# Feed-forwards of a retention and gated-delta trunk as 2x2x2 block products with seven products, down projection in four groups

## The chip, the cores and the metric

The kernel runs on one core of one Trainium2 chip. The metric is the device time of one execution in microseconds (us). A core has five engines that run their own instruction streams and wait for each other by semaphores: PE (TensorE, the matmuls), DVE (VectorE), ACT (ScalarE), POOL (GpSimd) and SP (SyncE, which here only issues DMAs). SBUF is the on-chip memory of 128 partitions, PSUM the eight accumulator banks that PE writes. All values are float32. A matmul here takes "fp32r" operands: each value is split into a high end, which is a rounded copy, and a low end, which is the value less that copy.

## What is computed

Two layers, each with two half-step SwiGLU feed-forwards around a mixer (retention in the first, gated delta rule in the second), on 520 tokens: 512 of a prompt and 8 samples. Cut to what matters here:

```python
D_MODEL, D_FF = 1024, 2816
def _swiglu(x, w_gu, w_down):
    a, b = jnp.split(x @ w_gu, 2, axis=-1)
    return (jax.nn.silu(a) * b) @ w_down
for i in range(DEPTH):                      # DEPTH = 2
    x = x + 0.5 * _swiglu(_rmsnorm(x, norm_g[i, 0]), ffn_gu[i, 0], ffn_down[i, 0])
    x = x + mixer(_rmsnorm(x, norm_g[i, 1]))    # retention, then gated delta
    x = x + 0.5 * _swiglu(_rmsnorm(x, norm_g[i, 2]), ffn_gu[i, 1], ffn_down[i, 1])
return _rmsnorm(x, final_g), states
```

## The kernel before

Activations lie transposed: model dimension on the partitions (8 tiles of 128), the 520 tokens along the row, in two halves of 260 (`HALF`). `plan()` lists ten phases in order: gate/up and down of feed-forward 0, retention, gate/up and down of feed-forwards 1 and 2, gated delta, gate/up and down of feed-forward 3. All engines walk this list; the order of their work is the order of the code.

Weights come in slots of at most 16 tiles of 128x128 (1 MB), two slots in turn. SP loads a slot into `raw`, ACT copies it to the high end `wh` (`split`, L1328, one instruction of 2048 columns, L1333), DVE subtracts to give the low end `wl` (`split`, L1669, L1672), and PE uses it. A slot of gate/up holds one gate tile column and one up tile column (8 tiles each), a slot of down holds half of a column of `w_down` (11 tiles, 1408 columns). So gate/up is 22 slots and down 16 slots a feed-forward.

On PE, `products` (L736) does for each weight tile three terms (high x high, high x low, low x high) for both halves of the tokens: six matmuls of 260 columns (L743), accumulated in two banks. That makes 22 x 96 + 8 x 132 = 3168 matmuls a feed-forward. After a gate and an up column DVE scales both by the norm's `rinv` (L2258), ACT applies Silu (L1632), DVE multiplies (L2261), ACT and DVE split the product into `hh` and `hl` (L1635, L2263). After a down column DVE adds into `x` (L2276), ACT and DVE make the next stage's scaled `xh` and `xl` (L1651, L1678), ACT squares (L1655) and POOL adds the squares (`sum_squares`, L548); the next stage's norm comes from that sum. POOL has no other work in the feed-forwards.

The mixers also use `split`, `products` and `in_products` (L934), and POOL does elementwise work in them: sums of squares (L588), masks and state decays (`add` in `gdn_body`, L643).

## Time and profile before

| | |
|---|---|
| median of 3 runs | 2621.64 us (2612.52 to 2621.98) |
| profiled execution, first to last instruction | 2619.2 us |
| PE busy | 2572.6 us, 98% of the span |
| DVE busy | 1264.2 us, 48% |
| ACT busy | 821.0 us, 31% |
| POOL busy | 300.5 us, 11% |
| mean granted PE clock | 0.990 of full speed |

The profiled execution is 2.4 us shorter than the median. Busy time of an engine is the union of its instructions. A timeline or chain row gives the start in us from the span's start, then its length in us. A row of a stretch gives busy us and instructions of PE, PEld (weight loads), DVE, ACT and POOL in that order. A row by line and form gives line, engine, operation, tiles, shapes and count, then busy us and the mean duration of one in ns, then the idle time before it and what ended most of it.

### The profile page before, as it was taken

The numbers are of one execution on the slowest core, as the hardware profiler recorded it, in microseconds if no ns is written. First come the engines' busy times: TensorE is split into PE (matmuls) and PEld (weight loads), VectorE is DVE, ScalarE is ACT, GpSimd is POOL, SyncE is SP. The second block draws the span as 40 slices with busy tenths as digits, with TensorE's granted clock in tenths as the row PEclk, the third lists the DMA queues.
The fourth block names the chain that finished last, engine by engine and source line by source line (L and its number), as shares of the span: only waits on it lengthen the run. The fifth ranks groups of instructions, "written<-read, shape, count | busy, mean of one in ns | idle before, by whom it ended". The sixth has DMA issues, their size and how long they took to land.

```text
span 2619.2 us, 48630 instructions
## 1 busy us (share of the span) xinstructions
PE 2572.6 (98%) x20575; PEld 2484.8 (95%) x20575; DVE 1264.2 (48%) x1584; ACT 821.0 (31%) x1042; POOL 300.5 (11%) x307
## 2 busy tenths in 40 slices
PE   8999999999999999999999999999999998999998
PEld 8999999898989899999999999989998998999998
DVE  5444334646464654443244443377557755444422
ACT  4222222424242432222232222244433344222222
POOL 1000010202020210000000000002530353000000
PEclk9999999999999999999999999999999999999999
DMA  4332334524242333332343323321122111323232
GB/s 131 96 96 76 88 93 141 185 86 177 93 173 97 137 91 87 96 86 78 97 111 91 96 82 89 104 84 52 49 66 87 36 49 53 97 84 93 78 91 74
DMA packets 340333, 246.73 MB, mean 94 GB/s; under 512 B 9428, under 2 KB 320908, under 8 KB 340208
## 3 DMA queue, kind: packets, MB, share of 16 engines
q1 hardware_dynamic: 325856, 197.32, 25.6%
q0 software_dynamic: 14352, 47.58, 5.0%
q8 instruction: 99, 1.62, 0.3%
q14 instruction: 26, 0.21, 0.0%
HBM read 218.81 MB, written 26.05 MB: 93 GB/s over the span
## 4 chain that ended last, share of the span: by engine, by line
PE 95%; DVE 3%; ACT 1%; issue 0%; DMA 0%; SPq 0%; ACTq 0%; DVEq 0%
PE ps L743 61%; PE ps L934 17%; PE ps L1118 5%; PE ps L828 1%; PE ps L851 1%; PE ps L837 1%; PE ps L1062 1%; PE ps L1128 1%; PE ps L783 1%; PE ps L1099 1%; DVE wl L1672 1%; PE ps L1075 1%; PE ps L993 0%; DVE xl L1678 0%; DVE cv L2012 0%
## 5 line engine op out<-in xcount | busy, mean ns | idle before, releaser
L743 PE MATMUL ps<-xh,wh 128*128 128x260 f32 x2816 | 569.0, 283 | 3.7 <-DVE gate L2258 1.5
L743 PE MATMUL ps<-xh,wl 128*128 128x260 f32 x2816 | 568.3, 284 | 0.0
L743 PE MATMUL ps<-xl,wh 128*128 128x260 f32 x2816 | 567.5, 283 | 0.0
L1672 DVE TENSOR_TENSOR wl<-raw,wh 128x2048 fp32r<-128x2048 f32 (+1 forms) x204 | 428.7, 2102 | 266.7 <-ACT wh L1333 266.5
L1333 ACT ACTIVATE wh<-raw 128x2048 fp32r<-128x2048 f32 (+1 forms) x204 | 354.5, 1738 | 343.2 <-PE ps L743 189.2
L743 PEld LDWEIGHTS ps<-xh,wh 128*128 128x128 f32 x2816 | 435.4, 189 | 5.8 <-issue 2.7
L743 PEld LDWEIGHTS ps<-xh,wl 128*128 128x128 f32 x2816 | 435.1, 189 | 0.0
L743 PEld LDWEIGHTS ps<-xl,wh 128*128 128x128 f32 x2816 | 433.8, 189 | 0.0
L743 PE MATMUL ps<-hh,wh 128*128 128x260 f32 x1408 | 284.4, 283 | 0.0
L743 PE MATMUL ps<-hh,wl 128*128 128x260 f32 x1408 | 283.1, 282 | 0.0
L743 PE MATMUL ps<-hl,wh 128*128 128x260 f32 x1408 | 282.8, 282 | 0.0
L934 PE MATMUL ps<-xh,wh 128*128 128x260 f32 x1280 | 271.1, 294 | 1.7 <-DVE rot L1727 0.8
L934 PE MATMUL ps<-xh,wl 128*128 128x260 f32 x1280 | 261.3, 286 | 0.0
L934 PE MATMUL ps<-xl,wh 128*128 128x260 f32 x1280 | 261.1, 286 | 0.0
L2258 DVE TENSOR_TENSOR up<-ps,rinv 128x520 f32<-128x520 f32 x88 | 61.5, 699 | 382.6 <-PE ps L743 382.6
L743 PEld LDWEIGHTS ps<-hl,wh 128*128 128x128 f32 x1408 | 217.1, 188 | 0.0
L743 PEld LDWEIGHTS ps<-hh,wl 128*128 128x128 f32 x1408 | 216.9, 188 | 0.0
L743 PEld LDWEIGHTS ps<-hh,wh 128*128 128x128 f32 x1408 | 216.6, 188 | 0.2
L934 PEld LDWEIGHTS ps<-xh,wh 128*128 128x128 f32 x1280 | 201.7, 193 | 15.5 <-issue 9.7
L1635 ACT ACTIVATE hh<-up 128x520 f32 (+1 forms) x88 | 56.3, 640 | 467.5 <-DVE up L2261 467.5
L934 PEld LDWEIGHTS ps<-xl,wh 128*128 128x128 f32 x1280 | 202.1, 193 | 0.0
L934 PEld LDWEIGHTS ps<-xh,wl 128*128 128x128 f32 x1280 | 202.0, 193 | 0.0
(372 smaller groups left out, 2857.8 us busy)
## 6 DMA issues: line engine op xcount, KB each, us to landing
raw<-in_ffn_gu_dram SPq DMA_DIRECT2D x176, 512.0 KB, 4.9
raw<-in_ffn_down_dram SPq DMA_DIRECT2D x64, 384.0 KB, 3.5
raw<-in_ret_w_in_dram SPq DMA_DIRECT2D x48, 512.0 KB, 4.4
raw<-in_ffn_down_dram SPq DMA_DIRECT2D x64, 320.0 KB, 3.9
s_ring<-in_state_ret_dram POOLq DMA_DIRECT2D x32, 512.0 KB, 6.2
out_dram<-s_ring POOLq DMA_DIRECT2D x32, 512.0 KB, 3.4
raw<-in_gdn_w_in_dram SPq DMA_DIRECT2D x32, 512.0 KB, 4.5
raw<-in_ret_w_out_dram SPq DMA_DIRECT2D x16, 512.0 KB, 3.8
```

Source lines behind the costliest of these rows:

```text
L743: m_ = nc.tensor.matmul(ps[:, 2 * q + h, 0:HALF], w_, v[:, kt0 + t, h * HALF:(h + 1) * HALF], start=b_, stop=e_)
L783: m_ = nc.tensor.matmul(o, rk[:, t, jb * P:(jb + 1) * P], rq[:, t, jb * P:SEQ], start=t == 0, stop=t == 1)
L828: m_ = nc.tensor.matmul(ps[:, 4 + e, jb * P:SEQ], vtok[:, jb, e * P:(e + 1) * P], pt[:, off[jb]:off[jb] + SEQ - P * jb], start=jb == 0, st ...
L837: m_ = nc.tensor.matmul(ps[:, 4 + t, :], ktok[:, jb, t * P:(t + 1) * P], vtok[:, jb, :], start=jb == 0, stop=jb == 3)
L851: m_ = nc.tensor.matmul(ps[:, 7, e * DEC + b:e * DEC + b + 1], weighed(b)[:, e * P:(e + 1) * P], ones[:, 0:1], start=True, stop=True)
L934: m_ = nc.tensor.matmul(ps[:, 2 * q + h, 0:HALF], w_, v[:, t, h * HALF:(h + 1) * HALF], start=t == 0 and n == 0, stop=t == KT - 1 and n == 2)
L1062: m_ = nc.tensor.matmul(ps[:, bank, h * P:(h + 1) * P], column(h).broadcast_to([P, P]), right, start=True, stop=True)
L1118: m_ = nc.tensor.matmul(ps[:, bank, h * P:(h + 1) * P], left[:, h, :], right[:, h, :], start=True, stop=True)
L1333: nc.scalar.activation(wh[:, s, 0:cols], raw[:, s, 0:cols], ACT.Copy).then_inc(w_high, 1)
L1635: nc.scalar.activation(hh[:, j, :], up[:], ACT.Copy).then_inc(h_high, 1)
L1672: nc.vector.tensor_tensor(wl[:, s, 0:cols], raw[:, s, 0:cols], wh[:, s, 0:cols].bitcast(F32), ALU.subtract).then_inc(w_low, 1)
L2258: nc.vector.tensor_tensor(halves(t_[:]), pair(g), halves(rinv[:]), ALU.mult).then_inc(acc_free, 1)
```

## The change

The ten phases become two mixers and four calls `ffn(f)`, each a list of 38 jobs: 22 G jobs (one gate and one up column) and 16 D jobs (two columns of `w_down` over part of D_FF). The D jobs come in four groups of four, each group after the G jobs that made its part of the hidden values: after 6, 12, 18 and 22 G jobs, with 2, 3, 3 and 3 pairs of hidden tiles (`kp` below). `x` is updated once a group.

A job is one 2x2x2 block product: the two halves of the tokens, two halves of the contraction, two output columns. Instead of eight products of blocks it makes seven, on sums and differences of blocks:

- PE: seven products of 3 x `kp` matmuls of 260 columns (`kp` is 4 in a G job). Partial results pile up in three banks, product after product; six is started when ACT has copied the content after product 1, and so on (`product`, `products_of`).
- POOL makes four sums or differences of weight blocks in a job, each of `kp` x 128 columns (`block_sum`), one sum of results (C22), differences of hidden values (T1 to T4, four for every two G jobs), and in D jobs an addition into `x` (XG).
- ACT and DVE split seven blocks of weights instead of four blocks' worth, in five instructions (groups A and L have two blocks, groups 1, 2 and 4 one), for the next job while PE works on this one. ACT copies four partial results from PSUM (m1, m5, u2, u3).
- DVE adds up results, scales the gate by `rinv` before Silu and after it (gr, sr), multiplies gate and up (hA, hB) and makes the low ends of the hidden blocks (w1, w2, w3).
- Ahead of a feed-forward the input is gained and mixed too (`before_ffn`: seven blocks for each of the four pairs of tiles), in the last four D jobs of feed-forward 1 for feed-forward 2 (`tile_done`).

SP issues two transfers a job as before. The feed-forward code is written out on all engines, without loops. Tiles get other addresses. The mixers' arithmetic stays. Cut to its core:

```diff
+NJ, KP, BLOCK = 38, 4, 4 * P
...
+def ffn_jobs():
+
+    out = []
+    for q0, q1, pairs_ in ((0, 6, (0, 1)), (6, 12, (2, 3, 4)), (12, 18, (5, 6, 7)), (18, 22, (8, 9, 10))):
+        out += [("G", q, (0, 1, 2, 3)) for q in range(q0, q1)] + [("D", m, pairs_) for m in range(4)]
+    return out
+
+
+JOBS = ffn_jobs()
...
+def products_of(j):
+
+    if j == 0:
+        return [(j, m) for m in (1, 5, 2, 6, 3, 7)]
+    if j == LATE:
+        return [(j, 1), (j - 1, 4)] + [(j, m) for m in (5, 6, 3, 2, 7)]
+    if j == NJ - 1:
+        return [(j, 1), (j, 2), (j, 5), (j, 6), (j - 1, 4), (j, 7), (j, 3), (j, 4)]
+    return [(j, 1), (j, 2), (j, 5), (j, 6), (j - 1, 4), (j, 3), (j, 7)]
+
...
+            gated = sb("gated", [P, 2, NTOK], stack=st)
+            kept = sb("kept", [P, 4, HALF], stack=st)
+            mixed = sb("mixed", [P, 2, BLOCK], stack=st)
+            parts = sb("parts", [P, 8, HALF], stack=st)
...
+            def block_sum(f, j, n):
+
+                r_, s_ = raw_blocks(f, j), mixed_block(j)
+                a11, a12, a21, a22 = r_[:, 0, :, 0, :], r_[:, 0, :, 1, :], r_[:, 1, :, 0, :], r_[:, 1, :, 1, :]
+                tt = nc.gpsimd.tensor_tensor
+                if n == "1":
+                    pool.wait_ge(f_landed[j % 2], job_landed(f, j))
+                    if j >= 2 or f == 2:
+                        pool.wait_ge(blk_low, blocks_split(*((f, j - 2) if j >= 2 else (f - 1, NJ - 2 + j)), "4"))
+                    m_ = tt(s_, a21, a22, ALU.add)
+                if n == "3":
+                    m_ = tt(a21, a11, a21, ALU.subtract)
+                if n == "2":
+                    pool.wait_ge(blk_low, blocks_split(f, j, "A"))
+                    pool.wait_ge(blk_sum, blocks_summed(f, j, "1"))
+                    m_ = tt(a11, s_, a11, ALU.subtract)
+                if n == "4":
+                    pool.wait_ge(blk_low, blocks_split(f, j, "1"))
+                    pool.wait_ge(blk_sum, blocks_summed(f, j, "2"))
+                    m_ = tt(s_, a12, a11, ALU.subtract)
+                m_.then_inc(blk_sum, 1)
...
+            def ffn(f):
...
+                for j in range(NJ + 1):
...
+                    if j:
+                        pool.wait_ge(ffn_a, FFN_A(f"u3.{b}", f))
+                        did(tt(kept[:, 2, :], kept[:, 2, :], kept[:, 3, :], ALU.add), f"C22.{b}")
+                    if odd:
...
+                        did(tt(parts[:, 6, :], parts[:, 5, :], parts[:, 2, :], ALU.subtract), f"T3.{e}")
...
+                        did(tt(parts[:, 7, :], parts[:, 5, :], parts[:, 1, :], ALU.subtract), f"T2.{e}")
+                        if j == LATE:
+                            fourth()
+                    if nxt:
+                        block_sum(*nxt, "2")
+                    if odd and j != LATE:
+                        fourth()
+                    if gated_b and not odd:
+                        v(f"hA.{b}")
+                        if e:
+                            v(f"w1.{e - 1}")
+                        did(tt(parts[:, 1, :], parts[:, 2, :], parts[:, 0, :], ALU.subtract), f"T1.{e}")
+                    if nxt:
+                        block_sum(*nxt, "4")
+                    if j > LATE:
+                        square_added(NORM_OUT[f], 2 * (j - LATE - 1))
+                    if j < NJ and not is_gate(j):
+                        xt = halves(x[:, 2 * JOBS[j][1], :])
+                        v(f"X11.{j}")
+                        v(f"X12.{j}")
...
+                        block_sum(*nxt2, "1")
+                        block_sum(*nxt2, "3")
+                    if f == 2 and j == LATE + 1:
+                        pool.wait_ge(ffn_t, FFN_T(f"4.{LATE - 1}", f))
...
+                def product(c, m, steps=None):
...
+                        if m in (1, 2, 5):
+                            bank_free(c, m)
+                        else:
...
+                        if kind == "D":
...
+                            m_ = nc.tensor.matmul(o, w_, r_, start=m in (1, 2, 5) and t == 0 and n == 0,
+                                                  stop=t == kp - 1 and n == 2, skip_group_check=m in (3, 4, 6, 7))
+                    if kp - 1 in steps:
...
+                for j in range(1, NJ):
+                    for c, m in products_of(j):
+                        product(c, m)
...
+            def x_gained(f, t):
...
+                nc.scalar.activation(x_parts(f, m)[:, at_:at_ + 3:2, :], halves(x[:, t, :]), ACT.Copy, scale=gains[:, g_:g_ + 1]).then_inc(xg_ready, 1)
...
+            def x_split(f, m, late):
...
+                nc.scalar.activation(xch[:, m, to_, :], x_parts(f, m)[:, from_, :], ACT.Copy).then_inc(xc_high, 1)
...
+            def block_split(f, j, group):
...
+                if j == 0 and f in (1, 3):
+                    act.wait_ge(parts_done, mixer_done(f, group in "4L"))
+                elif j or f:
+                    pf, pj = (f, j - 1) if j else (f - 1, NJ - 1)
+                    for m in {"A": (1, 2), "1": (5,), "2": (6,), "4": (3,), "L": (7,)}[group]:
+                        act.wait_ge(ffn_t, FFN_T(f"{m}.{pj}", pf))
+                    if group == "L" and (j >= 2 or f == 2):
+                        act.wait_ge(ffn_t, FFN_T(*((f"4.{j - 2}", f) if j >= 2 else (f"4.{NJ - 2 + j}", f - 1))))
+                nc.scalar.activation(split_ends(wh, j, group), split_from(f, j, group), ACT.Copy).then_inc(blk_high, 1)
...
+            def before_ffn(f, n):
...
+                    block_split(f, 0, "A")
+                    block_split(f, 0, "1")
...
+                act.wait_ge(acc_free, (0, phases[0].unit0 + phases[0].units - KT, 0, phases[1].unit0 + phases[1].units - KT)[f] + n + 1)
+                x_gained(f, n)
+                if n % 2:
+                    x_split(f, n // 2, False)
+                squared(NORM_IN[f], n)
...
+                    x_split(f, n // 2 - 1, True)
+                if n == KT - 1:
+                    block_split(f, 0, "4")
+                    x_split(f, n // 2, True)
+                    block_split(f, 0, "L")
...
+                def copy(j, name, m, slot):
...
+                    t_(f"{m}.{j}")
+                    nc.scalar.activation(kept[:, slot, :], ps[:, bank_of(j, m), 0:HALF], ACT.Copy, scale=1.0 if is_gate(j) else 0.5)\
+                        .then_inc(ffn_a, FFN_A.did(f"{name}.{j}"))
...
+                def h_split(n, e):
...
+                    p_({1: "T1", 2: "T2", 3: "T4"}[n] + f".{e}")
+                    nc.scalar.activation(hch[:, e % KP, to_, :], parts[:, from_, :], ACT.Copy).then_inc(ffn_a, FFN_A.did(f"k{n}.{e}"))
...
+                    if gated_b:
+                        v(f"gr.{b}")
+                        nc.scalar.activation(gated[:, JOBS[b][1] % 2, :], gated[:, JOBS[b][1] % 2, :], ACT.Silu).then_inc(ffn_a, FFN_A.did(f"silu.{b}"))
...
+                    high("A")
+                    copy(j, "m5", 5, 3)
+                    high("1")
...
+                    copy(j, "u2", 6, 1)
...
+                    high("2")
...
+                        first_slot(f)
...
+                    if ending:
...
+                        x_split(f + 1, m, True)
...
+            def tile_done(f, t):
...
+                    act.wait_ge(ffn_v, FFN_V(f"X22.{j}", f))
+                if f in (0, 2):
+                    scaled(f // 2, t)
+                if f == 1:
+                    x_gained(f + 1, t)
...
+            def x_mixed(f, m, n):
...
+                nc.vector.tensor_tensor(p_[:, to_, :], p_[:, i0, :], p_[:, i1, :], ALU.subtract).then_inc(xt_ready, 1)
...
+            def block_split(f, j, group):
+
+                dve.wait_ge(blk_high, blocks_split(f, j, group))
+                nc.vector.tensor_tensor(split_ends(wl, j, group), split_from(f, j, group), split_ends(wh, j, group).bitcast(F32),
+                                        ALU.subtract).then_inc(blk_low, 1)
...
+            def before_ffn(f, n):
+
+                m = n // 2
+                if n % 2:
+                    x_mixed(f, m, 0)
+                    if m:
+                        x_split(f, m - 1, True)
+                elif m:
+                    x_split(f, m - 1, False)
+                    for i in range(1, 4):
+                        x_mixed(f, m - 1, i)
...
+                    block_split(f, 0, "A12"[n - 4])
+                if n == KT - 1:
+                    x_split(f, m, False)
+                    for i in range(1, 4):
+                        x_mixed(f, m, i)
+                    block_split(f, 0, "4")
+                    x_split(f, m, True)
+                    block_split(f, 0, "L")
...
+                def scaled_by_norm(j, name):
...
+                    did(tt(mine(j), mine(j), rinv[:], ALU.mult), f"{name}.{j}")
...
+                def upper(j):
...
+                        did(tt(mine(j)[:, first], bank(j, 2), kept[:, 0, :], ALU.add), f"C11.{j}")
+                        return
...
+                def lower_second(j):
+
+                    p_(f"C22.{j}")
+                    if is_gate(j):
...
+                        did(tt(parts[:, 2 + 3 * (JOBS[j][1] % 2), :], kept[:, 2, :], mine(j)[:, second], ALU.mult), f"hB.{j}")
+                        return
+                    xt = x[:, 2 * JOBS[j][1] + 1, second]
+                    did(tt(xt, xt, kept[:, 2, :], ALU.add), f"X22.{j}")
...
+                def lower(j):
...
+                    t_(f"4.{j}")
...
+                        did(tt(parts[:, 3 * (JOBS[j][1] % 2), :], bank(j, 4), mine(j)[:, first], ALU.mult), f"hA.{j}")
+                        return
+                    xt = x[:, 2 * JOBS[j][1] + 1, first]
+                    did(stt(xt, bank(j, 4), 0.5, xt, ALU.mult, ALU.add), f"X21.{j}")
...
+                def h_split(n, e):
...
+                    did(tt(hcl[:, e % KP, to_, :], parts[:, from_, :], hch[:, e % KP, to_, :].bitcast(F32), ALU.subtract), f"w{n}.{e}")
...
+                for j in range(NJ + 1):
...
+                        if j == 1:
+                            mixer_stored(f)
+                        lower_second(b)
...
+                    low("A")
+                    low("1")
+                    if ending:
+                        tile_done(f, 2 * m)
+                    low("2")
+                    if odd:
+                        h_split(2, e)
+                    if j:
+                        lower(b)
+                    if j < NJ:
+                        upper_second(j)
+                    if j == NJ - 1 and f in (0, 2):
+                        split(phases[f // 2].slot0, 0)
+                    low("4")
+                    if j == 0:
...
+                        h_split(3 if odd else 1, e)
+                    low("L")
+                    if ending and f == 1:
+                        x_split(f + 1, m, True)
+
+            def tile_done(f, t):
+
+                m, j = t // 2, LATE + t // 2
+                if f in (0, 2):
+                    scaled_low(f // 2, t)
+                if f == 1 and t % 2 == 0:
+                    x_mixed(f + 1, m, 0)
...
```

## Rows read from the trace of the kernel before

**Rows 1.** Busy time of the engines over the whole span (page, part 1).

```profile
PE 2572.6 (98%) x20575; PEld 2484.8 (95%) x20575; DVE 1264.2 (48%) x1584; ACT 821.0 (31%) x1042; POOL 300.5 (11%) x307
```

**Rows 2.** The chain that ended last, shares of the span by line (page, part 4).

```profile
PE ps L743 61%; PE ps L934 17%; PE ps L1118 5%; PE ps L828 1%; PE ps L851 1%; PE ps L837 1%; PE ps L1062 1%; PE ps L1128 1%; PE ps L783 1%; PE ps L1099 1%; DVE wl L1672 1%; PE ps L1075 1%; PE ps L993 0%; DVE xl L1678 0%; DVE cv L2012 0%
```

**Rows 3.** Stretches: start:end, length, busy us (instructions) by engine, clock, DMA share, GB/s.

```profile
34.50:403.80 369.30, 369.28 (x3074) 369.30 (x3075) 143.98 (x139) 96.03 (x95) 9.62 (x7) 1.00 0.32 90
...
2232.90:2606.10 373.20, 373.12 (x3107) 372.78 (x3107) 139.12 (x138) 94.27 (x101) 8.51 (x7) 1.00 0.29 82
```

**Rows 4.** DVE by line and form, gate/up of feed-forward 0 (34.5 to 290 us).

```profile
L1672 DVE TENSOR_TENSOR wl<-raw,wh 128x2048 fp32r<-128x2048 f32 x20 | 45.9, 2293 | 19.9 <-ACT wh L1333 19.9
L2261 DVE TENSOR_TENSOR up<-up,gate 128x520 f32<-128x520 f32 x22 | 15.4, 701 | 2.3
L1672 DVE TENSOR_TENSOR wl<-raw,wh 128x1408 fp32r<-128x1408 f32 x3 | 4.9, 1626 | 5.3 <-ACT wh L1333 5.3
```

**Rows 5.** DVE by line and form, whole span: 256 columns from PSUM, and scaled_low.

```profile
L1678 DVE SCALAR_TENSOR_TENSOR xl<-x,gains,xh x18 | 13.7, 760 | 21.8 <-ACT xh L1651 21.8
L2078 DVE TENSOR_TENSOR x<-ps,x 128x256 f32<-128x256 f32 x16 | 6.6, 421 | 2.9 <-PE ps L1045 2.9
```

**Rows 6.** POOL by line and form, whole span.

```profile
L643 POOL TENSOR_TENSOR la<-d,gcon 128x512 f32<-128x512 f32 x24 | 30.4, 1279 | 5.7 <-DVE m L2108 5.3 <-PE ps L1118 0.4
L630 POOL MEMSET rst<- 40x520 f32 x2 | 1.1, 554 | 0.0
L657 POOL MEMSET gyl<- 40x256 f32 x2 | 0.7, 328 | 0.0
```

**Rows 7.** Timeline of POOL, then of DVE, around 474 us.

```profile
473.91 3.99 POOL L588 TENSOR_TENSOR osum<-osum,rot 128x512 f32<-128x512 f32 x1
...
473.82 0.74 DVE L1786 SCALAR_TENSOR_TENSOR spare<-s_ring,rq,spare 128x512 f32<-128x512 f32 x1
474.48 2.28 DVE L1672 TENSOR_TENSOR wl<-raw,wh 128x2048 fp32r<-128x2048 f32 x1
```

**Rows 8.** Timeline of POOL, then of DVE, around 1814 us.

```profile
1814.16 1.80 POOL L643 TENSOR_TENSOR lb<-d,gcon 128x512 f32<-128x512 f32 x1 [1.97 <-DVE d L2100]
...
1814.84 1.67 DVE L2108 TENSOR_TENSOR m<-ident,la 128x512 f32<-128x512 f32 x1
```

**Rows 9.** Timeline of POOL, then of DVE, around 465 us.

```profile
465.70 1.26 POOL L588 TENSOR_TENSOR osum<-osum,rot 128x512 f32<-128x512 f32 x1 [1.47 <-ACT rot L1389]
...
464.96 2.73 DVE L1773 SCALAR_TENSOR_TENSOR s_ring<-ps,rk,s_ring 128x512 f32<-128x512 f32 x4 [5.19 <-PE ps L821]
```

**Rows 10.** Timeline of POOL, two instructions back to back.

```profile
1825.46 1.27 POOL L643 TENSOR_TENSOR la<-d,gcon 128x512 f32<-128x512 f32 x1 [0.69 <-DVE m L2108]
1826.69 1.27 POOL L643 TENSOR_TENSOR lb<-d,gcon 128x512 f32<-128x512 f32 x1
```

**Rows 11.** Timeline of PE: first and last of twelve matmuls into one bank.

```profile
1933.55 0.36 PE L1043 MATMUL ps<-gyh,wh 128*128 128x256 f32 x1
...
1934.94 0.28 PE L1045 MATMUL ps<-gyh,wl 128*128 128x256 f32 x1
```

**Rows 12.** Stretches with a lowered PE clock (columns as in Rows 3).

```profile
18.80:24.00 5.20, 5.20 (x24) 5.20 (x25) 5.20 (x6) 3.40 (x7) 4.77 (x4) 0.50 0.73 202
...
611.30:621.40 10.10, 10.10 (x49) 10.10 (x48) 8.23 (x14) 5.82 (x5) 1.07 (x2) 0.50 0.82 305
```

**Rows 13.** ACT by line and form, whole span.

```profile
L1333 ACT ACTIVATE wh<-raw 128x2048 fp32r<-128x2048 f32 x140 | 266.8, 1905 | 218.3 <-PE ps L934 144.4 <-PE ps L743 64.3 <-PE ps L1045 9.7
L1632 ACT ACTIVATE gate<-gate 128x520 f32<-128x520 f32 x88 | 56.2, 639 | 268.5 <-DVE gate L2258 268.5
```

**Rows 14.** Longest pieces of the chain in order of time (start us, us, what).

```profile
18.73 9.86 PE ps L743 x60
...
34.52 369.24 PE ps L743 x3072
```

**Rows 15.** DMA issues: KB each, median us from issue to landing.

```profile
raw<-in_ffn_gu_dram SPq DMA_DIRECT2D x176, 512.0 KB, 4.9
```

960 lines of the change are left out of this document (603 added, 357 removed).

## Prediction, made before the changed kernel ran

> **What bounds the kernel now.** I read the page first: PE is busy 98% of the span, DVE 48%, POOL 11% [rows 1], and the chain that ended last runs through PE's matmul lines, L743 alone 61% [rows 2]. Then the stretches: a feed-forward after its first slot takes 369.3 us, with 3074 matmuls and PE busy throughout, while DVE works 144 us, ACT 96 us and POOL under 10 us [rows 3]. (There are four such stretches. Feed-forward 3 takes 373.2 us, as it holds the output transposes too.) So a matmul costs 369.3 / 3074 = 0.120 us, nothing else is near, and any matmul taken away would count in full, until another engine becomes the bound. The prediction is about that "until".
>
> **What the change takes away.** A G job needs 7 x 4 x 3 = 84 matmuls instead of 96, a D job 63 (42 with two pairs). A feed-forward has 22 x 84 + 12 x 63 + 4 x 42 = 2772 instead of 3168, 396 fewer, worth 47.6 us, and 190 us over the four. PE needs 10.1 us for a G job, 7.6 us for a D job, 5.0 us for the short D job. The products are no longer in alternating banks; twelve matmuls of 256 columns into one bank follow each other every 0.126 us [rows 11], so I price that at nothing, with at most 0.1 us at each change of bank (0.7 us a job, under PE's slack below).
>
> **What it adds on DVE.** A 2048-column subtraction takes 2.29 us, 1408 columns 1.63 us, 520 columns 0.70 us [rows 4]: 1.04 ns a column and 0.16 us. 256 columns take 0.42 us [rows 5]. So 1024 columns are 1.22, 780 are 0.97, 512 are 0.69, 260 are 0.43 us. In a G job, of the instructions that read two operands from SBUF: low ends of weights 2 x 1.22 + 3 x 0.69 = 4.5; gr and sr 1.4; hB 0.43; w1 to w3 (0.70 + 0.97 + 0.70 for two jobs) 1.2. Sum 7.5 us. C11, C12 and hA read one operand from PSUM, another 1.3 us.
>
> **What it adds on POOL.** An undisturbed 512-column operation takes 1.28 us [rows 6]; back to back they start every 1.23 us [rows 10], so the record's length is real. 260 columns don't occur: between 0.64 (half) and 1.28 us; memsets of 520 and 256 columns take 0.55 and 0.33 us [rows 6], nearly no fixed part, so I take 0.70. A G job has four block sums, C22 and on average two T's: 4 x 1.27 + 3 x 0.70 = 7.2 us.
>
> **The two together.** Each alone fits under PE's 10.1 us. But they don't run together. At 473.9 us a POOL addition that takes 1.26 us elsewhere [rows 9] took 3.99 us: DVE was in two-operand instructions, the split L1672 until 476.76, and POOL ended 1.14 us after that [rows 7]. The other way round, DVE's L2108, 512 columns, took 1.67 us instead of 0.69: POOL ended at 1815.96, DVE 0.55 us later [rows 8]. Where DVE reads one operand from PSUM, four instructions L1773 beside POOL's 1.26 us, neither is longer [rows 9]. So an operation of POOL on SBUF and a DVE one with two SBUF operands exclude each other for their length, 0.55 us of DVE or 1.14 us of POOL for 512 columns. The Trainium skill (SBUF — State Buffer, SBUF: two separate sides) says the same: the port pair shared by the two is an exclusive lock held for the whole instruction, and this trace agrees with the 3.99 and 1.67 us above. Before, this cost nothing as POOL had no work in the feed-forwards. Now a G job holds the port for 7.5 + 7.2 = 14.7 us at full lengths, and for 5794 columns x 1.07 ns + 2828 x 2.2 ns = 12.4 us at the holds, packed without a pause. Both are over PE's 10.1 us.
>
> Between them I decide by following the order of the code. From DVE's low end A of the next job: block sum 2 (POOL) 1.2, its high end (ACT) 0.63, its low end 0.7, in odd jobs w2 1.1, hA 0.43, T4 or T1 0.7, block sum 4 1.2, high end 0.63, low end 0.7, gr, w3 or w1, low end L, sr, hB, C11 and low end A again 0.6 + 0.6 + 1.1 + 0.6 + 0.4 + 0.4 + 1.1, and into that POOL's sums 1 and 3, C22, T3, T2 push in for some 3 us in even and 4.5 us in odd jobs, since POOL's order puts them ahead of block sum 2. That gives about 15.6 us for an odd and 13.8 us for an even job, 14.7 us on average. PE isn't in this loop: it waits for the weights' low ends and for hA to free its bank. ACT (1.9 us for 2048 columns, 0.64 for 520 [rows 13]) needs 0.21 us + 0.83 ns a column, 7.4 us a job, with slack.
>
> A D job by the same rows: DVE 2 x 0.96 + 3 x 0.56 + 0.43 = 4.0, POOL 4 x 0.98 + 0.70 + 1.29 (XG) = 5.9, together 9.9 us, packed 8.2; I take 9.4, as fewer of its waits leave the port free. The short one 7.8, packed 6.3; I take 7.3. Both are over PE's times.
>
> **The sum**, against the profiled 2619.2 us. A feed-forward after its first job: 21 x 14.7 + 12 x 9.4 + 4 x 7.3 = 451 us. Against 3 x 369.3 + 373.2 that is +323 us. The last four D jobs carry more: two scaled_low (0.76 [rows 5]) and two square sums (1.27) in feed-forwards 0 and 2, 4.1 us a job, 16 us each; in 1 the mixing of the next input, two square sums, 4 x 0.43 + 0.70 + 1.52 on DVE, 6.5 us a job, 26 us; in 3 some 14 us: +72. Jobs with no successor drop their splits and sums: -20. The head of feed-forwards 0, 1 and 3 holds the port for 35 us (DVE 16 x 0.43 + 4 x 2.2 + 4.5, POOL 7 x 1.3 + 4 x 1.27). In feed-forward 0 that ends near 45 us, where now the steady stretch starts at 34.5 us [rows 14]; in 1 and 3 it lies partly beside the mixer's last projection: +10, +6, +8. Loads are 1 MB a job in two transfers of 4.9 us [rows 15] with over 9 us from the freed slot to the first use: nothing; if that cover failed it would be 1 or 2 us at the four returns from D to G jobs. Straight-line code: the mixers' written-out PE code already runs without gaps in the chain, nothing. Total 2619 + 323 + 72 - 20 + 24 = 3018, with the 2.4 us to the median 3020 us.
>
> **Rivals.** (1) Packed: DVE and POOL hand the port over without a pause and the queues run ahead of the loop above. Then 21 x 12.4 + 12 x 8.2 + 4 x 6.3 = 384 us a feed-forward, +55, edges +58 - 16 + 24: 2740 us. For it: instructions queue while they wait. Against: in-order queues on both, and a loop of single hand-overs. (2) Faster: the exclusion is as rare as in the mixers, PE stays the bound, and the 190 us come off: 2619 - 190 + 24 = 2453 us. It decides at a G job of 10.1 us of port time; the sums are over it even packed, so only a mistake in what holds the port saves it. (3) PE's clock falls. PE would be idle about 4.6 us of every G job. At the start and in the retention there are stretches with a granted clock of 0.50, that is 1.2 GHz, and a matmul of 260 columns then takes 5.2 / 24 = 0.217 us [rows 12], so a G job is 18.2 us of PE. If every second job were at that level the four feed-forwards would cost some 260 us more: 3280 us; at that level throughout, 3550 us. Up to 0.175 us a matmul it hides in PE's slack. The Trainium skill (TensorE: Matmul & The Clock Gate, Part 1: The HAM clock gate) has the clock fall when PE idles. In both stretches of [rows 12] PE is recorded busy, so no row here shows how the clock takes idle gaps between full products. (4) No change: port time near 11 us a job, about 2620 us; nothing points to it.
>
> **How the numbers follow.** The forecast, 2790 to 3140 us, 3020 us likeliest: 0.72. Packed, 2700 to 2790 us: 0.12. Faster: 0.05. Within 0.5% (about what a measurement of this kernel can tell from no change): 0.03. Clock or further waits, over 3140 us: 0.08. The range 2720 to 3140 us takes the forecast and most of the packed case, 0.82. Slower by over 0.5%: 0.92.
>
> **What would show it.** Right: PE busy about 70% of a feed-forward stretch, 12 to 15 us from one G job to the next; block sums on POOL well over 1.27 us on average and DVE's 512-column low ends well over 0.69 us; PE's waits ended by DVE; the mixers unchanged. Wrong: both at their undisturbed lengths, or PE busy over 95%. A clock well under 1.0 in the feed-forwards shows rival 3. The prediction fails if the record's lengths of POOL include time in which the port is free.

## The result, and the profile after

| | us | runs |
|---|---|---|
| before, median | 2617.1 (2606.6 to 2622.0) | 4 |
| changed, median | 3150.7 (3147.3 to 3152.8) | 4 |
| ratio | 1.205, 95% interval 1.202 to 1.209 | |
| span of the profiled execution, changed | 3150.2 | |

The forecast was 3020 us in a range of 2720 to 3140, slower with 0.92. The sign and the mechanism in the gate/up jobs came as forecast. The time lies 11 us above the range. The profiled span is 132 us over the sum of 3018, and the down jobs are what was sized worst.

Busy times and the chain of the changed kernel (page, parts 1 and 4):

```profile
PE 2610.0 (83%) x18991; PEld 2462.9 (78%) x18991; DVE 2084.3 (66%) x2788; ACT 1321.7 (42%) x2334; POOL 1528.8 (49%) x1307
...
PE 35%; POOL 28%; issue 24%; DVE 9%; ACT 3%; POOLq 0%; DMA 0%; ACTq 0%; SPq 0%; DVEq 0%
```

Beside [rows 1] PE issues 1584 matmuls fewer and yet is not busy for less time: a matmul of 260 columns is recorded with a mean of 298 to 312 ns in L1546, against 282 to 284 in L743 before. The timelines show records of 0.42 us at the lower clock and of 0.56 us behind a wait, instead of 0.28. POOL's time is five times the former 300 us and it is 28% of the chain, where [rows 2] had PE's lines nearly alone.

The same stretch of the middle of feed-forward 0 in both kernels, before first (columns as in rows 3):

```profile
100.00:400.00 300.00, 300.00 (x2500) 300.00 (x2499) 113.98 (x108) 77.17 (x77) 9.62 (x7) 1.00 0.32 91
```

```profile
100.00:400.00 300.00, 232.34 (x1702) 224.14 (x1703) 206.22 (x265) 130.19 (x251) 191.37 (x160) 0.93 0.23 68
```

PE finishes 1702 matmuls in the time of 2500. No engine is busy throughout: DVE 206 and POOL 191 of 300 us, and both work on the same things by turns. The longest waits of the changed kernel say so as a ring (engine, line, for whom: us in total, times, longest):

```profile
DVE wl L2114 <- ACT wh L1661: 423.8, 237, 2.4
ACT wh L1661 <- POOL raw L709: 374.1, 142, 4.5
POOL raw L709 <- DVE wl L2114: 368.9, 112, 9.7
```

On POOL L703 is block sum 1, L705 sum 3, L709 sum 2, L713 sum 4, L756 C22, L774 T1, L761 T3, L763 T2. POOL by line and form (busy us, mean ns of one):

```profile
L756 POOL TENSOR_TENSOR kept<-kept 128x260 f32<-128x260 f32 x152 | 161.8, 1065 | 0.0
L709 POOL TENSOR_TENSOR raw<-mixed,raw 128x512 f32<-128x512 f32 x88 | 145.7, 1655 | 212.1 <-DVE wl L2114 212.1
L703 POOL TENSOR_TENSOR mixed<-raw 128x512 f32<-128x512 f32 x88 | 141.0, 1602 | 19.7 <-DVE yl L2425 19.7
...
L713 POOL TENSOR_TENSOR mixed<-raw 128x512 f32<-128x512 f32 x88 | 112.6, 1280 | 7.5 <-DVE wl L2114 3.8
...
L763 POOL TENSOR_TENSOR parts<-parts 128x260 f32<-128x260 f32 x44 | 67.7, 1539 | 0.0
...
L774 POOL TENSOR_TENSOR parts<-parts 128x260 f32<-128x260 f32 x44 | 32.7, 743 | 74.7 <-DVE parts L2212 74.7
```

The same instruction on the same number of columns takes 1280 ns at L713 and 1655 at L709, 743 ns at L774 and 1539 at L763. What sets the difference is seen in the timeline of one job, POOL and then DVE (start, length, both in us):

```profile
180.00 1.73 POOL L703 TENSOR_TENSOR mixed<-raw 128x512 f32<-128x512 f32 x1
181.70 1.74 POOL L705 TENSOR_TENSOR raw<-raw 128x512 f32<-128x512 f32 x1
183.40 1.21 POOL L756 TENSOR_TENSOR kept<-kept 128x260 f32<-128x260 f32 x1
```

```profile
179.31 1.28 DVE L2114 TENSOR_TENSOR wl<-raw,wh 128x512 fp32r<-128x512 f32 x1 [1.84 <-ACT wh L1661]
180.51 0.42 DVE L2215 SCALAR_TENSOR_TENSOR x<-ps,x 128x260 f32<-128x260 f32 x1
180.85 0.41 DVE L2189 TENSOR_TENSOR gated<-ps,kept 128x260 f32<-128x260 f32 x1
181.19 1.10 DVE L2114 TENSOR_TENSOR wl<-mixed,wh 128x512 fp32r<-128x512 f32 x1
182.21 1.78 DVE L2169 TENSOR_TENSOR gated<-gated,rinv 128x520 f32<-128x520 f32 x1
```

DVE's L2114 ends at 180.59, POOL's L703 1.14 us later at 181.73, the next L2114 0.56 us after that at 182.29, POOL's L705 1.15 us later at 183.44, and L2169 0.55 us after that at 183.99. These are the 1.14 and 0.55 us of [rows 7, 8], now as a relay. The two DVE operations that read one operand from PSUM (L2215, L2189) lie in the middle of POOL's 1.73 us and keep 0.42 us, as L1773 did in [rows 9].

The pace of the jobs is the distance between two C22. POOL's timeline in the second group, C22 alone (the first row is job 10's, 312.95 is job 20's):

```profile
183.40 1.21 POOL L756 TENSOR_TENSOR kept<-kept 128x260 f32<-128x260 f32 x1
196.75 1.18 POOL L756 TENSOR_TENSOR kept<-kept 128x260 f32<-128x260 f32 x1
212.67 1.19 POOL L756 TENSOR_TENSOR kept<-kept 128x260 f32<-128x260 f32 x1
226.64 1.19 POOL L756 TENSOR_TENSOR kept<-kept 128x260 f32<-128x260 f32 x1
242.00 1.21 POOL L756 TENSOR_TENSOR kept<-kept 128x260 f32<-128x260 f32 x1
254.08 1.19 POOL L756 TENSOR_TENSOR kept<-kept 128x260 f32<-128x260 f32 x1
...
312.95 1.20 POOL L756 TENSOR_TENSOR kept<-kept 128x260 f32<-128x260 f32 x1
```

13.4, 15.9, 14.0, 15.4, 12.1 us. The ten jobs of six gate/up and four down jobs take 312.95 - 183.40 = 129.6 us; forecast were 6 x 14.7 + 4 x 9.4 = 125.8. That is near, but by luck: by job (the distance from the C22 before to its own), six gate/up jobs take 79.9 us where 88.2 were forecast, and four down jobs 49.7 where 37.6 were. A part of this is where the line is drawn, as a group's first down job (15.6 us) also holds the end of the last gate/up job; the down jobs behind it still take 10.9 to 12.2 us.

The 132 us that the sum missed lie at two places, by the same distances in all four feed-forwards. From the first C22 to the last a feed-forward takes 481.0, 490.1, 486.8 and 483.5 us, 1941 in all where 1855 were forecast (+87): the first group with its short down jobs 114.5 us instead of 102.7 (+47 over four), the two middle groups 129.6 instead of 125.8 (+30), the last four gate/up jobs 50 instead of 59 (-35), the last four down jobs 248 in all instead of 202 (+45, before rounding). And the starts and ends of the feed-forwards, mixers between them included, cost 70 us over before where 24 were forecast (+46). The same 1941 us by kind of job, over all four feed-forwards:

| jobs | number | forecast, us each | measured, us each | in all against the sum |
|---|---|---|---|---|
| gate/up, after the first | 84 | 14.7 | 13.4 | -113 |
| short down | 16 | 7.3 | 10.9 | +58 |
| other down | 32 | 9.4 | 12.4 | +96 |
| last four down | 16 | 12.7 | 15.5 | +45 |

So the down jobs cost 199 us more than the sum gave them, and gate/up jobs that were priced too high hide 113 of it.

### The profile page after: what moved, and what is told of

Read it like the earlier page. It is cut to its first block, busy times and chain, and to the rows that moved or that the text cites. A ratio compares the mean times of both kernels' runs of the same rounds, so it can differ in the third digit from the quotient of the medians.

```text
span 3150.2 us, 49953 instructions
## 1 busy us (share of the span) xinstructions
PE 2610.0 (83%) x18991; PEld 2462.9 (78%) x18991; DVE 2084.3 (66%) x2788; ACT 1321.7 (42%) x2334; POOL 1528.8 (49%) x1307
## 4 chain that ended last, share of the span: by engine, by line
PE 35%; POOL 28%; issue 24%; DVE 9%; ACT 3%; POOLq 0%; DMA 0%; ACTq 0%; SPq 0%; DVEq 0%
PE ps L1178 15%; POOL raw L709 6%; POOL mixed L703 5%; POOL kept L756 4%; PE ps L1546 4%; PE ps L1362 4%; POOL mixed L713 4%; DVE wl L2114 3%; POOL x L784 2%; PE ps L984 2%; POOL raw L705 2%; POOL parts L763 2%; DVE parts L2101 2%; ACT wh L1661 1%; PE ps L1073 1%
## 5 line engine op out<-in xcount | busy, mean ns | idle before, releaser
L1546 PE MATMUL ps<-xch,wh 128*128 128x260 f32 x2464 | 768.4, 312 | 258.2 <-DVE parts L2212 98.0
L1546 PE MATMUL ps<-xcl,wh 128*128 128x260 f32 x2464 | 747.9, 304 | 0.0
L1546 PE MATMUL ps<-xch,wl 128*128 128x260 f32 x2464 | 747.7, 303 | 0.0
L1546 PEld LDWEIGHTS ps<-xch,wh 128*128 128x128 f32 x2464 | 519.8, 211 | 288.9 <-DVE parts L2212 109.2
L2114 DVE TENSOR_TENSOR wl<-raw,wh 128x1024 fp32r<-128x1024 f32 (+4 forms) x456 | 535.4, 1174 | 235.8 <-ACT wh L1661 233.3
L1546 PE MATMUL ps<-hch,wh 128*128 128x260 f32 x1232 | 383.7, 311 | 200.5 <-ACT kept L1708 72.9
L1546 PEld LDWEIGHTS ps<-xcl,wh 128*128 128x128 f32 x2464 | 520.1, 211 | 0.2
L1546 PEld LDWEIGHTS ps<-xch,wl 128*128 128x128 f32 x2464 | 518.2, 210 | 0.0
L1546 PEld LDWEIGHTS ps<-hch,wh 128*128 128x128 f32 x1232 | 252.4, 205 | 228.0 <-ACT kept L1708 87.2
L709 POOL TENSOR_TENSOR raw<-mixed,raw 128x512 f32<-128x512 f32 (+2 forms) x152 | 219.3, 1442 | 368.9 <-DVE wl L2114 368.9
L2114 DVE TENSOR_TENSOR wl<-mixed,wh 128x512 fp32r<-128x512 f32 (+2 forms) x304 | 257.8, 848 | 190.9 <-ACT wh L1661 190.5
L1546 PE MATMUL ps<-hch,wl 128*128 128x260 f32 x1232 | 367.9, 299 | 0.0
L1546 PE MATMUL ps<-hcl,wh 128*128 128x260 f32 x1232 | 367.6, 298 | 0.0
L1178 PE MATMUL ps<-xh,wh 128*128 128x260 f32 x1280 | 269.9, 292 | 4.4 <-DVE wl L2085 2.9
L1178 PE MATMUL ps<-xl,wh 128*128 128x260 f32 x1280 | 259.6, 285 | 0.0
L1178 PE MATMUL ps<-xh,wl 128*128 128x260 f32 x1280 | 259.5, 285 | 0.0
L1546 PEld LDWEIGHTS ps<-hcl,wh 128*128 128x128 f32 x1232 | 252.9, 205 | 0.0
L1546 PEld LDWEIGHTS ps<-hch,wl 128*128 128x128 f32 x1232 | 252.2, 205 | 0.0
L703 POOL TENSOR_TENSOR mixed<-raw 128x512 f32<-128x512 f32 (+2 forms) x152 | 214.4, 1411 | 19.7 <-DVE yl L2425 19.7
```

The lines of the kernel that those rows point to most:

```text
L703: m_ = tt(s_, a21, a22, ALU.add)
L709: m_ = tt(a11, s_, a11, ALU.subtract)
L1178: m_ = nc.tensor.matmul(ps[:, 2 * q + h, 0:HALF], w_, v[:, t, h * HALF:(h + 1) * HALF], start=t == 0 and n == 0, stop=t == KT - 1 and n == 2)
L1546: m_ = nc.tensor.matmul(o, w_, r_, start=m in (1, 2, 5) and t == 0 and n == 0, stop=t == kp - 1 and n == 2, skip_group_check=m in (3, 4, 6 ...
L2114: nc.vector.tensor_tensor(split_ends(wl, j, group), split_from(f, j, group), split_ends(wh, j, group).bitcast(F32), ALU.subtract).then_inc ...
```

## The experiments

All ten are edits of the changed kernel. They ran in three sets (e1 to e4, e5 to e8, e9 and e10), each with before on the same chip: 2612.6, 2617.0 and 2614.0 us. The changed kernel has a set of its own, with before at 2617.1. Gains in us compare medians of different sets, so one of 3 us says nothing, and those of 12 and 17 us (e9, e3) need the traces beside them: the intervals of their ratios to before overlap with the changed kernel's.

**e2_low_psum: the low ends of weights don't meet POOL.** DVE keeps its sizes, its order and its waits.

```diff
-                nc.vector.tensor_tensor(split_ends(wl, j, group), split_from(f, j, group), split_ends(wh, j, group).bitcast(F32),
+                other = split_ends(wh, j, group).bitcast(F32)
+                if inside and not (f == 3 and j > LATE):
...
+                    other = ps[:, 3, 0:kp * P].rearrange("p (t c) -> p t c", c=P)
...
+                nc.vector.tensor_tensor(split_ends(wl, j, group), split_from(f, j, group), other,
```

`inside` holds for all low ends that are made during a feed-forward's jobs, so also for the first jobs and, but for feed-forward 3, the last four.

> All operations keep their number, sizes, order and waits; only the low ends of the weights on DVE read their second operand from an unused PSUM bank instead of SBUF (the weights' low ends are left out of the computation). A 260 or 512-column operation of DVE takes the same time either way. Port theory: 4.5 of 14.7 us of a G job leave the port, 10.2 are left: G jobs 11 to 12 us, 2650 to 2850 us, POOL's sums back under 1.4 us. Chain theory (the waits' chain of hand-overs is too long by itself, exclusion or not): unchanged within 2% of 3151 us. Clock theory: unchanged too, as PE has the same work.

Measured: 2947.7 us (2947.1 to 2951.8), 203 us less than the changed kernel, ratio to before 1.128 (1.125 to 1.131). The low ends and POOL's sums, by form; the first row is the changed kernel's, the others e2's:

```profile
L2114 DVE TENSOR_TENSOR wl<-mixed,wh 128x512 fp32r<-128x512 f32 x176 | 170.5, 969 | 136.4 <-ACT wh L1661 136.2
...
L2120 DVE TENSOR_TENSOR wl<-mixed,ps 128x512 fp32r<-128x512 f32 x170 | 116.4, 685 | 138.6 <-ACT wh L1661 137.0
...
L709 POOL TENSOR_TENSOR raw<-mixed,raw 128x512 f32<-128x512 f32 x88 | 113.3, 1288 | 208.7 <-DVE wl L2120 208.3
...
L763 POOL TENSOR_TENSOR parts<-parts 128x260 f32<-128x260 f32 x44 | 32.9, 747 | 0.0
```

The low end falls from a mean of 969 ns to 685, and on POOL sum 2 and T2, of which nothing was changed, from 1655 to 1288 and from 1539 to 747 ns. An operand's place on DVE sets POOL's time: that shows the exclusion. The time stays above this theory's 2650 to 2850 us; DVE's other passes still have two operands in SBUF (e5 takes that up); a theory without the exclusion had no gain at all.

**e5_all_psum: no pass of DVE in the middle jobs meets POOL.**

```diff
-                    did(tt(mine(j), mine(j), rinv[:], ALU.mult), f"{name}.{j}")
+                    if 1 < j < LATE:
+                        did(tt(halves(mine(j)), halves(mine(j)), from_psum(2), ALU.min), f"{name}.{j}")
+                    else:
+                        did(tt(mine(j), mine(j), rinv[:], ALU.mult), f"{name}.{j}")
```

and so for hB, X22 and w1 to w3, on top of e2.

> As e2_low_psum, and between job 2 and the last four also the products with the norm's factor, hB, X22 and the low ends of hidden values take their second operand from PSUM bank 3 (two multiplications are minima, so that what is computed is not the reference; sizes, order and waits stay). No VectorE pass of these jobs then has both operands in SBUF. If the rest of the loss is still two-SBUF passes on both engines (in e2 the 520-column products still take 1088 ns and the low ends of hidden values 1225, beside POOL's sums), the gate/up job falls from 12.2 us to about 11 and the time from 2948 to 2790 to 2870 us. If what is left is POOL's own chain and the hand-overs, the time stays at 2900 to 2948.

Measured: 2849.3 us (2841.1 to 2855.0), another 98 us less, inside the first range. The 520-column product falls from 1088 ns in e2 to 688. So the exclusion that e5 takes away is worth 3150.7 - 2849.3 = 301 us, 267 of them in jobs 3 to 33 of the feed-forwards (1568 against 1301 us by the distances of C22); the rest comes from the first and the last jobs, which e2's part of the edit reaches. But nothing excludes POOL any more in jobs 3 to 33, and their gate/up jobs still take 10.9 us on average where PE needs 10.1.

**e1_small_sums: POOL's four block sums on one column.** From job 2 of each feed-forward on the sums of weights are left out but for that column; the instructions and all waits stay.

```diff
+                if j > 1:
+                    a11, a12, a21, a22, s_ = (v_[:, 0:1, 0:1] for v_ in (a11, a12, a21, a22, s_))
```

> From job 2 of each feed-forward on, POOL's four block sums work on one column instead of up to 512 (the weight sums are left out of the computation; all waits stay). Port theory (POOL and DVE exclude each other and that sets the pace): a G job loses 5.1 us of port time, 9.6 us are left, so PE's 10.1 us bound it: 2440 to 2560 us, PE busy over 90% in the feed-forwards, DVE's 512-column low ends back near 0.7 us. Clock theory (idle PE falls to 1.2 GHz and that sets the pace): the same kernel would recover only if the clock does, so the two agree here; a result above 2800 us would speak against both and for DVE and ACT alone being too slow.

Measured: 2717.0 us (2712.0 to 2732.2), ratio 1.039 (1.036 to 1.042). 434 us come back, the largest single share, but the expected 2440 to 2560 us is missed by far: the kernel stays slower than before with this work gone.

**e8_small_sums_low_psum and e10_small_sums_all_psum: e1 with e2, and e1 with e5.** They tell whether a PSUM operand is a gain by itself, and what the order of the change reaches.

> As e1_small_sums, and VectorE's weight low ends take their second operand from PSUM, as in e2_low_psum, where that gave 203 us. If it gave them because it met POOL's block sums less, then with the sums gone it gives 0 to 60 us: 2655 to 2717 us. If a pass with one operand from PSUM is simply shorter, whatever POOL does, it gives 130 us or more again: below 2590 us.

> e5_all_psum and e1_small_sums together: block sums of one column, and no VectorE pass with two operands in SBUF between job 2 and the last four. It is the floor that the order of this change has without the sums and without VectorE's long passes. e8_small_sums_low_psum gave 2616 us at 10.0 us a gate/up job. If VectorE still paces that one, the gate/up job falls to 9.0 to 9.5 us and the time to 2540 to 2590 us. If PE or the hand-overs do, it stays at 2600 to 2617. Either way the forecast of a faster kernel (2453 us, block sums free) lies below what this order reaches.

Measured: 2616.5 us (2613.9 to 2619.9), ratio 1.000 (0.998 to 1.001), and 2613.2 us (2610.5 to 2615.9), ratio 1.000 (0.999 to 1.002). With the sums gone the low ends' place gives 101 us, half of the 203; neither expected range holds it. Without the sums POOL still has C22, the T's and XG, which meet DVE: in e1 T2 takes 1540 ns, in e8 747. A pass with an operand in PSUM isn't shorter by itself: the 512-column low end takes 684 ns in e8, and the same pass on SBUF operands 0.69 us where POOL doesn't hold it up (182.33 us in e1's timeline, last section). e10 adds 3 us, nothing beside the intervals: the second of its cases. The stretch of e8 says why:

```profile
100.00:400.00 300.00, 287.56 (x2362) 284.33 (x2361) 221.58 (x364) 186.67 (x354) 100.72 (x220) 1.00 0.34 101
```

PE is busy 288 of 300 us at the full clock, and ten jobs (six gate/up, four down) take 90.8 to 92.1 us in the two middle groups, where PE needs 6 x 10.1 + 4 x 7.6 = 91.0. So PE is the bound again there, and the kernel is still no faster than before. e5 and e10 also tell what the sums cost without exclusion: 2849 - 2613 = 236 us. The gate/up jobs from job 3 on fall from 10.9 to 9.9 us by it and the middle down jobs from 10.1 to 8.0. I put that down to the sums' own length in the ring of waits above (1.29 us for sum 2 and for sum 4, each followed by ACT's high end and DVE's low end, with C22, T's, sums 1 and 3 in POOL's queue ahead of them); which of these links counts was not tried one by one, and PE's own need of 91.0 us for ten jobs ends the gain. The 301 and the 236 are the two steps from the changed kernel to e10, 537 us in all. In the other order the steps are 434 (e1) and 104 us: much of what the sums cost, they cost by exclusion, and the two shares belong to one order of taking away.

**e4_sums_dve: the four sums on DVE instead of POOL,** in DVE's order right behind the low end that each waits for. Nothing is left out.

```diff
-                tt = nc.gpsimd.tensor_tensor
+                tt = nc.vector.tensor_tensor
...
                     def low(group):
                         if nxt:
                             block_split(*nxt, group)
+                            if j != LATE and group in "A1" or j == LATE and group == "A":
+                                for n in {"A": "24" if j == LATE else "2", "1": "4"}[group]:
+                                    block_sum(*nxt, n)
+                            if nxt2 and group == "L":
+                                block_sum(*nxt2, "1")
+                                block_sum(*nxt2, "3")
```

> The four block sums of a job move from POOL to DVE, 0.69 us each for 512 columns instead of 1.28 us of POOL; POOL keeps C22, T1 to T4 and XG. Nothing is left out. Port theory: a G job needs DVE 7.5 + 1.3 + 2.8 = 11.6 us and POOL 2.1 us of port: 12 to 13.5 us a G job, total 2880 to 3050 us, faster than the change but not than the kernel before. Chain theory without exclusion: DVE alone is as loaded as DVE and POOL side by side were not, so slower than 3151 us, 3200 us or more.

Measured: 2828.8 us (2827.6 to 2829.7), ratio 1.082 (1.079 to 1.085), 322 us less than with the sums on POOL and better than the 2880 to 3050 expected. DVE's busy time of the middle stretch:

```profile
100.00:400.00 300.00, 268.89 (x2072) 264.85 (x2072) 287.36 (x437) 163.96 (x303) 83.71 (x74) 0.94 0.30 88
```

and the four sums by form (sum 2, 1, 4 and 3):

```profile
L2094 DVE TENSOR_TENSOR raw<-mixed,raw 128x512 f32<-128x512 f32 x88 | 77.1, 876 | 2.9
...
L2088 DVE TENSOR_TENSOR mixed<-raw 128x512 f32<-128x512 f32 x88 | 73.1, 831 | 0.0
...
L2098 DVE TENSOR_TENSOR mixed<-raw 128x512 f32<-128x512 f32 x88 | 60.9, 692 | 3.0
L2090 DVE TENSOR_TENSOR raw<-raw 128x512 f32<-128x512 f32 x88 | 59.8, 680 | 0.0
```

Here one engine is the bound, DVE with 287 of 300 us. It is the better place for the sums, as a sum takes 0.68 to 0.88 us instead of 1.28 to 1.66 and needs no hand-over, and the kernel is still 8% slower than before.

**e3_two_terms: PE leaves out the product of the high ends,** 56 matmuls a gate/up job instead of 84; and **e7_small_sums_two_terms,** the same on top of e1.

```diff
-                        for n, (w_, r_) in enumerate(((hi_w, high), (hi_w, low), (lo_w, high))):
+                        for n, (w_, r_) in enumerate(((hi_w, low), (lo_w, high))):
...
-                                                  stop=t == kp - 1 and n == 2, skip_group_check=m in (3, 4, 6, 7))
+                                                  stop=t == kp - 1 and n == 1, skip_group_check=m in (3, 4, 6, 7))
```

> PE leaves out the term high x high in the feed-forwards: 56 matmuls a G job instead of 84; all else stays. Port theory with PE off the loop: 3151 us within 1%, at most 40 us less where PE was waited for (heads, first D job of the last group). Clock theory: PE at 1.2 GHz was part of the pace; with a third less work it falls by 5% or more, under 3000 us.

> As e1_small_sums (block sums of one column from job 2 on), and PE leaves out the product of high ends, as in e3_two_terms: 56 matmuls a gate/up job instead of 84. If without the sums PE is the pace (its busy time was 367 of 400 us there), the gate/up job falls from 10.4 us to 8 or 9 and the time from 2717 to 2560 to 2640 us. If VectorE with ScalarE sets it there too, the time stays at 2690 to 2717.

Measured: e3 3133.3 us (3125.1 to 3138.7), 17 us less than the changed kernel; e7 2679.3 us (2672.2 to 2692.8), 38 us less than e1, between its two cases and nearer to the second. The stretches, e3 first:

```profile
100.00:400.00 300.00, 195.21 (x1139) 184.43 (x1138) 206.18 (x266) 130.75 (x254) 190.88 (x160) 0.80 0.24 68
```

```profile
100.00:400.00 300.00, 220.26 (x1497) 207.68 (x1498) 234.64 (x350) 170.47 (x334) 128.34 (x209) 0.90 0.32 94
```

In e3, with a third of the feed-forwards' matmuls gone and an even lower clock, 0.80, DVE and POOL do the same work in the same 300 us to within 0.1 and 0.5 us. PE and its clock don't set the middle jobs of the changed kernel: all but 5 of the 19 us between the first and the last C22 come off the last four down jobs. They are little of the starts and ends too: mixers included, these take 1204 instead of 1209 us. In e1 PE is busy 276 of 300 us, and taking a third of its work away gives only 1.4%: it isn't what holds e1 back either, but for those 38 us.

**e6_older_pairs: the last down group takes hidden pairs made earlier,** 7, 8 and 9, so that its first job doesn't wait for the last gate/up jobs.

```diff
-    for q0, q1, pairs_ in ((0, 6, (0, 1)), (6, 12, (2, 3, 4)), (12, 18, (5, 6, 7)), (18, 22, (8, 9, 10))):
+    for q0, q1, pairs_ in ((0, 6, (0, 1)), (6, 12, (2, 3, 4)), (12, 18, (5, 6, 7)), (18, 22, (7, 8, 9))):
```

> The last down group multiplies hidden pairs 7, 8 and 9 instead of 8, 9 and 10; nothing else changes (so pair 10 is made and not used, pair 7 is used twice). The first down job of that group takes 21.6 to 24.5 us where 13.4 were forecast. If it waits for the last pair's hidden values (hC, their splits on ScalarE and VectorE), it falls to 13 to 17 us and the kernel by 25 to 40, to 3110 to 3125 us. If it is long because of what VectorE and POOL do in it for the jobs behind, it stays at 21 to 24 and the time within 8 us of 3150.

Measured: 3122.4 us (3120.2 to 3124.1), 28 us less. PE's waits around that job in feed-forward 0, the changed kernel first and then e6:

```profile
485.02 0.56 PE L1546 MATMUL ps<-hch,wh 128*128 128x260 f32 x1 [5.16 <-DVE hcl L2221]
```

```profile
479.49 0.39 PE L1546 MATMUL ps<-hch,wh 128*128 128x260 f32 x1 [0.49 <-DVE parts L2212]
482.11 0.58 PE L1546 MATMUL ps<-xch,wh 128*128 128x260 f32 x1 [1.27 <-ACT kept L1708]
```

The 5.2 us for the hidden blocks' low ends are gone, and the distance of the two C22 falls from 24.0 to 16.2 us. So the drain of the last pair costs 28 us over the four feed-forwards.

**e9_small_heads: the differences at the starts shortened,** by taking `x_mixed` over one column for the tile pairs where that is possible (three pairs in feed-forward 2, one in the others).

```diff
-                nc.vector.tensor_tensor(p_[:, to_, :], p_[:, i0, :], p_[:, i1, :], ALU.subtract).then_inc(xt_ready, 1)
+                c_ = slice(0, 1) if m == 3 or f == 2 and m else slice(0, HALF)
+                nc.vector.tensor_tensor(p_[:, to_, c_], p_[:, i0, c_], p_[:, i1, c_], ALU.subtract).then_inc(xt_ready, 1)
```

> The changed kernel, whose four differences of the mixed input (x_mixed, VectorE) are taken over one column instead of 260 for three of the four tile pairs in the third feed-forward and for the last pair in the others; sizes of everything else, order and waits stay. The starts of the feed-forwards cost 70 us where 24 were forecast. If VectorE's chain of differences and low ends sets them, the stretch from the second feed-forward's last gather to the third's first, 23.2 us now, falls by 5 to 8 us, and the kernel to 3135 to 3145 us. If the multiplications set it (the clock granted there was 0.56), or ScalarE's copies, nothing moves by more than 2 us: 3147 to 3153.

Measured: 3138.7 us (3133.9 to 3140.5), 12 us less. The three differences of the last pair at the border of feed-forwards 1 and 2, changed kernel first:

```profile
1592.80 2.19 DVE L2101 TENSOR_TENSOR parts<-parts 128x260 f32<-128x260 f32 x3 [0.80 <-ACT parts L1639]
1596.35 1.51 DVE L2109 TENSOR_TENSOR xcl<-parts,xch 128x1300 fp32r<-128x1300 f32 x1 [1.35 <-ACT xch L1645]
```

```profile
1581.95 0.50 DVE L2102 TENSOR_TENSOR parts<-parts 128x1 f32<-128x1 f32 x3 [0.80 <-ACT parts L1639]
1583.81 1.51 DVE L2110 TENSOR_TENSOR xcl<-parts,xch 128x1300 fp32r<-128x1300 f32 x1 [1.35 <-ACT xch L1645]
```

What is saved on the differences (2.19 to 0.50 us) comes through to the low ends in full, 3.55 us after the first difference before and 1.86 now. From the last C22 of feed-forward 1 to the first of 2 it is 18.9 instead of 23.2 us, 4.3 less and a little under the 5 to 8 expected. So this start is a chain in which each difference counts, and the first C22 of feed-forward 0, behind one shortened pair, comes 2.3 us earlier too. How the rest of the 70 us at starts and ends divides was not tried.

## Why the prediction was right or wrong

- **What the change takes away: right.** 18991 matmuls instead of 20575 are 1584 = 4 x 396 fewer; with the sums and the low ends out of the way PE paces ten jobs at 90.8 to 92.1 us, 91.0 by the forecast (e8). So no cost of adding product after product in one bank is seen, where the prediction took nothing.
- **The durations: right but for one.** DVE's 512 columns take 0.69 us and 1024 columns 1.22 undisturbed (175.66 us in the changed kernel's timeline, 1.21 on average in e8). POOL's 260 columns take 0.74 us, where 0.70 was taken between 0.64 and 1.28. The Trainium skill (GPSIMD Engine Reference, 3.1 Elementwise — side-by-side cycle accounting) gives about 2.6 cycles an element for such an operation, 2.2 ns at the 1.2 GHz that it counts with; 1.28 us for 512 columns and 0.74 for 260 have a slope of 2.1 ns a column here, which agrees.
- **The exclusion: right, and shown.** Forecast from three overlaps [rows 7 to 9], it is worth 301 us (e2 and e5). The Trainium skill (SBUF — State Buffer, SBUF: two separate sides) limits the lock to passes of VectorE in a 2-port mode or with two SBUF inputs, the latter only against a GpSimd operation that reads SBUF. This case agrees: with one operand of DVE in PSUM, POOL's time for sum 2 falls from 1655 to 1288 ns.
- **The order of the code as a loop: right as a mechanism, near in its size partly by luck.** The forecast of 15.6 and 13.8 us for odd and even gate/up jobs met 15.9 and 14.0 in the middle of a group, and that is why rival 1 failed: packed port time alone (2740 us) needs hand-overs without a pause, and e5, in which the middle jobs have no exclusion at all, still takes 2849 us. But the terms written for the loop add up to 16.6 and 14.0 us, not 15.6 and 13.8: 15.3 on average, which over 84 jobs would have made the forecast 50 us longer. And in the middle groups the first two gate/up jobs and the last take 9.2, 13.3 and 12.1 us, so that the average is 13.4 where 14.7 were summed: 113 us too much.
- **Down jobs: mis-sized by 154 us, the step that failed.** The sum took 9.4 us for a down job and 7.3 for a short one, between their packed port time (8.2 and 6.3) and their port time at full lengths (9.9 and 7.8), "as fewer of its waits leave the port free". They took 12.4 and 10.9 us, more than the port is held even at full lengths. I had followed the loop of hand-overs through a gate/up job only and left the down jobs at port time. The same two causes act in them: without the exclusion they take 10.1 and 9.3 us (e5), without the sums as well 8.0 and 7.0 (e10). That the total missed by 132 us and not by more is owed to the 113 us too much in the gate/up jobs.
- **Last down jobs: mis-sized by 45 us.** The first of them waits for the hidden values of the last two gate/up jobs, which no step of the sum had: 28 us (e6). The sum put only additional instructions there. The remaining 17 us were not traced; the price of 9.4 us for the job itself is probably a part of them.
- **Starts and ends: mis-sized by 46 us.** I priced the starts as port time that ends near 45 us in feed-forward 0; the first C22 comes at 59.7 us, where before PE ran steadily from 34.5 us [rows 14]. They are a chain of single steps for each of four tile pairs (gain on ACT, differences on DVE, high ends on ACT, low ends on DVE), which e9 shows for the last pair at one start: 1.7 us saved on the differences are 1.7 us at the low ends. A third less work for PE shortens starts and ends by 4 us in all (e3), so the matmuls and their clock are little of it.
- **Rival 3, the clock: it fell, but less than the rival had it, and in the slack.** The middle stretch has a mean granted clock of 0.93 where before had 1.00; at the first start the mean from 18 to 60 us is 0.58 against 0.93. In that start's timeline matmuls of 260 columns begin every 0.22 us where PE runs, as in [rows 12]. In the middle jobs it costs next to nothing: e3 takes PE's work down by a third at clock 0.80 for 17 us. The rival's time of 3280 us needed the lower level for every second job. Between the two levels of 0.5 and 1.0, a mean of 0.93 is about a seventh of the time.
- **Rival 2, faster: out of reach for a second reason.** It said that the 190 us come off if the exclusion is rare, 2453 us. e8 has no sums and no low ends in the way, PE as the bound, and 2616 us. From first to last C22 its feed-forwards take 346 to 361 us, 69 us less in all than the four stretches of before, of which [rows 3] has two, and the starts and ends give 65 of them back. PE's need alone would have been 323 us each. Of the 119 us above it, 79 lie in the last four down jobs (11 to 14 us each on average where PE needs 7.6) and 41 in the first group with its short down jobs (79 to 83 us for nine jobs, 70.5 by PE's need).

```profile
18.00:60.00 42.00, 20.57 (x100) 18.78 (x101) 35.89 (x36) 22.92 (x33) 22.20 (x16) 0.58 0.09 25
```

That row is the changed kernel's start: 100 matmuls in 42 us, and DVE busy for 36 of them; before had 312 matmuls in the same stretch. No version that was run beats the kernel before.

## What to carry to other kernels

Work that saves a bounding engine 8% is worth that only if what it adds stays out of the loop by which the next job is prepared: add up the loop in the order of the queues for every kind of job, the short and the last ones too, and not the busy times of the engines. Two-operand passes of VectorE and GpSimd on SBUF count as work of one engine; before such work is given to an idle GpSimd, price it there with VectorE's passes in front of it, and try it on VectorE as well (here 322 us better). A saving inside a stretch that a pipeline must be filled for is paid for at each start and end: even with the sums gone and DVE's low ends out of POOL's way (e8) 65 us at starts and ends undid the 69 us that were left of the saving inside the feed-forwards. And a sum that comes out right in one place is to be held against the trace kind by kind: here 113 us too much in one kind of job hid most of 154 us too little in another.
